# A hybrid mixer step on one core: the last RMSNorm of all rows moved into the last expert, into free weight slots

## The chip, the cores and the metric

One Trainium2 chip, one of its cores. The time is device microseconds of one launch of the whole program on that core; the median of the runs is what counts. A profile is one execution of the same program with the hardware profiler on.

## The reference, cut to what matters

One layer is computed for 1024 latent rows and 256 context rows of 1024 floats (all float32). After a mixer (Fourier and retention heads) comes an expert-choice MoE: each of 16 experts picks the 128 latent rows and 32 context rows with its highest gates, and its weighted output is added to these rows. A row can be picked by several experts or by none. Then every row is normalised once more.

```python
def rmsnorm(x, g):
    r = lax.rsqrt(jnp.mean(x * x, axis=-1, keepdims=True) + EPS)
    return (x * r) * g

gates, idx = lax.top_k(aff.T, cap)                 # per expert: cap rows
xs = ht[idx]
y = (silu(xs @ w_gate) * (xs @ w_up)) @ w_down * gates[..., None]
x = x + gate2 * zeros.at[idx].add(y)               # over 16 experts
y_prompt, y_sample = rmsnorm(xp, final_g), rmsnorm(xs, final_g)
```

## The kernel before, in words

The program is raw blocks, one after the other, each with a hand-written instruction list per engine and semaphores between them; every block ends with all engines meeting. Up to the router (the first 840 us) the rows are mixed, normalised and stored twice in device memory: `xn2` (input of the experts) and `acc` (the residual, to which expert outputs are added). The MoE block takes the rest but for the last 30 us.

In the MoE block an expert is 11 steps (`STEPS`) of 256 hidden columns. Per step SP loads three 1 MB weight tiles (gate, up, down) into one of four slots of `rawW` (`RING`, slot = step mod 4). ACT and DVE split the weights into a high and a low fp32r part (`gate_up_hi` L1205 and `gate_up_lo` L1210, `down_hi` L1527 and `down_lo` L1594), PE does gate and up (`gate_up`, L1420, and for context rows L1433), ACT applies SiLU (`sg` L1552, `sgc` L1558), DVE multiplies, PE transposes the hidden tile (`psT` L1463/1464), ACT and DVE split it (`hidden_hi` L1522, `hidden_lo` L1586), and PE does the down product one step late (`down`, L1446 and L1454), counted by the semaphore `f_d`. The down product of the last step of the last expert stands behind the loop, alone. Then ACT copies half of the context sums (`take_context_half` L1533), DVE applies the gates (`take_y`, L1607 to L1612), and POOL adds the 128 + 64 half rows into `acc` with two indirect DMAs that accumulate (`scatter`, L1662). POOL also gathers the input rows of the next expert into `xgS`/`xgP` (`gather`, L1655). The expert loop is `experts`: the first and the last expert are written out, the others are a hardware loop.

A last block then does the RMSNorm over ten tiles of 128 rows: SP loads each tile of `acc` (L1691) and `final_g` broadcast to all partitions (L1693); ACT squares and sums (L1708); POOL scales, adds EPS (L1714) and raises to -0.5 (L1716); DVE multiplies by that and by `final_g` (L1723); SP stores the tile (L1699).

Of the kernel before, what the change touches and what calls it, by code (L numbers as in the profile page):

```python
# [30 lines left out]
N = N_S + N_P  # L31
TS, TP = N_S // P, N_P // P
# [52 lines left out]
def build(nc, io):  # L85
    ctx = ExitStack()
    with ctx:
        sems = []

        def sem(name):  # L90
            sems.append(nc.alloc_semaphore(name=name))
            return sems[-1]

        def sb(name, shape, dt=F32, c=ctx):
            return c.enter_context(nc.sbuf_tensor(name, shape, dt))
# [836 lines left out]
        with ExitStack() as c:  # L932
# [26 lines left out]
            d_st = [sem("d_st0"), sem("d_st1")]  # L959
            d_tr, d_h2, d_lg, d_lc = sem("d_tr"), sem("d_h2"), sem("d_lg"), sem("d_lc")  # L960
            catv = catT.rearrange("(k p) n -> p k n", p=P)

            def schedule(eng, step):

# [247 lines left out]

        idxT = sb("idxT", [P, 48], I32)
        gT = sb("gT", [P, 48])
        with ExitStack() as c:
            mx = sb("mx", [P, T], F32, c)
            sm_ = sb("sm", [P, T], F32, c)
# [16 lines left out]
            with nc.Block() as block:  # L1234
# [39 lines left out]
                def _(dve):  # L1274
# [55 lines left out]
        with ExitStack() as c:  # L1330
# [17 lines left out]
            psS = ps("psS", [CS, 2, 512], c)  # L1348
            psP = ps("psP", [P, 512], c)
            X_AT, XS = 2, NK // 2  # L1350
            rows2 = [t.rearrange("n (a d) -> (n a) d", a=2) for t in (xn2, acc)]

            f_q, f_c = sem("f_q"), sem("f_c")
# [9 lines left out]

            f_si, f_yp, f_y, f_ys = sem("f_si"), sem("f_yp"), sem("f_y"), sem("f_ys")
            f_sc, f_free = sem("f_sc"), sem("f_free")

            def pair(t, e):

# [19 lines left out]
            with nc.Block() as block:  # L1388
                @block.sync
                def _(sp):  # L1390
                    sp.wait_ge(f_got, 32)

                    def load_down(e, i):
                        sp.wait_ge(f_d, STEPS * e + i - reuse(i) + 1)
                        load(sp, D_, e, i)

                    def body(e, first, last):
                        for i in range(STEPS):
                            s = STEPS * e + i
# [8 lines left out]
                    load_down(E - 1, STEPS - 1)  # L1408

                @block.tensor  # L1410
                def _(pe):
# [84 lines left out]
                def _(act):  # L1496
# [43 lines left out]
                    def body(e, first, last):  # L1540
                        for i in range(STEPS):
# [28 lines left out]
                    take_context_half(E)  # L1570

                @block.vector
                def _(dve):
# [29 lines left out]
                    def take_y(e):  # L1603
# [41 lines left out]
                    take_y(E)  # L1645

                @block.gpsimd
                def _(gp):
# [9 lines left out]
                    def scatter(e):  # L1658
# [4 lines left out]
                                                  compute_op=ALU.add).then_inc(f_sc, 16)  # L1663
                        gp.wait_ge(f_sc, 32 * e)

                    gather(0)

                    def body(e, first, last):
# [5 lines left out]
                            gp.sem_inc(f_free, 1)  # L1674

                    experts(gp, body)
                    scatter(E)

        with ExitStack() as c:  # L1680
            xf = sb("xf", [P, T, D], F32, c)
            gf = sb("gf", [P, D], F32, c)
            sq = sb("sqG", [P, 2, D], F32, c)
            ss, rs = sb("ssG", [P, T], F32, c), sb("rsG", [P, T], F32, c)
            g_g, g_x = sem("g_g"), a_x
            g_sq, g_ms, g_rs, g_y, g_out = sem("g_sq"), sem("g_ms"), sem("g_rs"), sem("g_y"), sem("g_out")
            with nc.Block() as block:  # L1687
                @block.sync
                def _(sp):
                    for t in range(T):  # L1690
                        sp.dma_start(xf[:, t, :], acc[t * P:(t + 1) * P, :]).then_inc(g_x[t], 16)  # L1691
                        if t == 0:
                            sp.dma_start(gf[:], io["final_g"].rearrange("(a d) -> a d", a=1).broadcast_to([P, D])  # L1693
                                         ).then_inc(g_g, 16)
                    for t in range(T):
                        sp.wait_ge(g_y, t + 1)
                        dst = (io["y_sample"][0, t * P:(t + 1) * P, :] if t < TS else
                               io["y_prompt"][0, (t - TS) * P:(t - TS + 1) * P, :])
                        sp.dma_start(dst, xf[:, t, :]).then_inc(g_out, 16)  # L1699
                    sp.wait_ge(g_out, 16 * T)  # L1700

                @block.scalar
                def _(act):
                    for t in range(T):
                        act.wait_ge(g_x[t], 32)
                        if t >= 2:
                            act.wait_ge(g_sq, t - 1)
                        act.activation(sq[:, t % 2, :], xf[:, t, :], ACT.Square, accum_out=ss[:, t:t + 1]).then_inc(g_sq, 1)  # L1708

                @block.gpsimd  # L1710
                def _(gp):
                    for t in range(T):
                        gp.wait_ge(g_sq, t + 1)
                        gp.tensor_scalar(ss[:, t:t + 1], ss[:, t:t + 1], 1.0 / D, EPS, ALU.mult, ALU.add).then_inc(g_ms, 1)  # L1714
                        gp.wait_ge(g_ms, t + 1)
                        gp.tensor_tensor(rs[:, t:t + 1], ss[:, t:t + 1], nhalf[:, 0:1], ALU.pow).then_inc(g_rs, 1)  # L1716

                @block.vector
                def _(dve):
                    dve.wait_ge(g_g, 16)  # L1720
                    for t in range(T):
                        dve.wait_ge(g_rs, t + 1)
# [24 lines left out]
```

## Time and profile before

| | us |
|---|---|
| median of 3 runs | 3174.97 (3174.19 to 3179.51) |
| the profiled execution, timed | 3178.7 |
| its span, first to last instruction | 3176.0 |
| PE busy of the span | 2915.9 (92%) |
| DVE busy | 1772.3 (56%) |
| ACT busy | 1574.4 (50%) |
| POOL busy | 435.5 (14%) |

The profile lists, per engine, what ran when, for how long, and what ended the idle time in front of it. Times in it are counted from the start of the span. A matmul's end is modelled; spans on POOL are rough. A register or semaphore instruction is not listed as busy.

### The profile page before, as it was taken

To read this page: it belongs to the slowest core of one execution; us is meant where nothing else is said; L and a number is where in the kernel's file an instruction comes from.
4 is the path that set the end of the run, shared out by engine and by line. 5 is a ranking of instruction groups with operands and counts; after the bars stand their busy time and mean duration, and the time that the engine had idled before them with its cause. 6 is when DMAs were issued, how large, how long until landed. Compare 5 with 4: busy or idle time off the path is not lost. (4 is left out here: it accounts for less than half of the span.)

```text
span 3176.0 us, 61303 instructions
## 1 busy us (share of the span) xinstructions
PE 2915.9 (92%) x23879; PEld 2200.5 (69%) x23879; DVE 1772.3 (56%) x2627; ACT 1574.4 (50%) x2473; POOL 435.5 (14%) x448
## 2 busy tenths in 40 slices
PE   5899998898399999999999999999999999999993
PEld 2799996587277767667676767667676767667772
DVE  2333331131667666666666666666666666666763
ACT  3322221133265656556565656556565656556652
POOL 3243331021201010101101010101101010101102
PEclk9999999898599999999999999999999999999996
DMA  9211102153577686868677686868678686868764
GB/s 385 76 41 35 34 17 78 50 175 119 196 238 253 232 293 218 295 228 270 229 262 261 229 290 210 295 232 272 230 256 266 229 291 205 295 234 274 249 237 147
DMA packets 483864, 668.99 MB, mean 211 GB/s; under 512 B 14689, under 2 KB 418993, under 8 KB 480562
## 3 DMA queue, kind: packets, MB, share of 16 engines
q1 hardware_dynamic: 476978, 644.45, 59.8%
q0 software_dynamic: 6656, 20.98, 2.6%
q8 instruction: 205, 3.36, 0.4%
q14 instruction: 25, 0.20, 0.0%
HBM read 633.39 MB, written 31.98 MB: 209 GB/s over the span
## 5 line engine op out<-in xcount | busy, mean ns | idle before, releaser
L1210 DVE TENSOR_TENSOR wGU_lo<-rawW,wGU_hi 128x1024 fp32r<-128x1024 f32 x700 | 824.9, 1218 | 74.3 <-ACT wGU_hi L1205 74.3
L1205 ACT ACTIVATE wGU_hi<-rawW 128x1024 fp32r<-128x1024 f32 x704 | 731.9, 1054 | 148.8 <-PE psGU L1420 139.7
L1420 PE MATMUL psGU<-wGU_hi,X_hi 128*128 128x512 f32 x1408 | 588.9, 418 | 54.4 <-issue 51.5
L1420 PE MATMUL psGU<-wGU_lo,X_hi 128*128 128x512 f32 x1408 | 568.4, 404 | 0.0
L1420 PE MATMUL psGU<-wGU_hi,X_lo 128*128 128x512 f32 x1408 | 567.7, 403 | 0.0
L1594 DVE TENSOR_TENSOR wD_lo<-rawW,wD_hi 128x1024 fp32r<-128x1024 f32 x352 | 415.2, 1220 | 63.1 <-ACT wD_hi L1527 63.1
L1586 DVE TENSOR_TENSOR hid_lo<-psT,hid_hi 128x256 fp32r<-128x256 f32 x176 | 74.5, 423 | 533.1 <-ACT hid_hi L1522 533.1
L1420 PEld LDWEIGHTS psGU<-wGU_hi,X_hi 128*128 128x128 f32 x1408 | 273.7, 194 | 124.5 <-issue 56.3
L1522 ACT ACTIVATE hid_hi<-psT 128x256 fp32r<-128x256 f32 x176 | 67.5, 384 | 576.6 <-PE psT L1464 576.2
L1527 ACT ACTIVATE wD_hi<-rawW 128x1024 fp32r<-128x1024 f32 x352 | 351.8, 1051 | 0.0
L1433 PE MATMUL psC<-rawW,Xc 128*32 128x128 f32 x11264 | 344.0, 274 | 0.0
L1433 PEld LDWEIGHTS psC<-rawW,Xc 128*32 128x32 f32 x11264 | 296.7, 110 | 64.4 <-issue 64.4
L1420 PEld LDWEIGHTS psGU<-wGU_hi,X_lo 128*128 128x128 f32 x1408 | 273.3, 194 | 65.1
L1420 PEld LDWEIGHTS psGU<-wGU_lo,X_hi 128*128 128x128 f32 x1408 | 274.2, 195 | 56.7
L1446 PE MATMUL psS<-wD_hi,hid_hi 128*128 128x512 f32 x704 | 238.4, 420 | 2.8 <-DVE wD_lo L1594 2.8
L1655 POOL DMA_INDIRECT xgS<-xn,gi x16 | 16.0, 1003 | 1610.4 <-DVE gi L1622 1583.2
L1446 PE MATMUL psS<-wD_lo,hid_hi 128*128 128x512 f32 x704 | 220.6, 395 | 0.0
L1446 PE MATMUL psS<-wD_hi,hid_lo 128*128 128x512 f32 x704 | 217.9, 391 | 0.0
L1662 POOL DMA_INDIRECT acc<-ysS,si x16 | 125.6, 7853 | 523.3 <-DVE ysP L1612 523.3
L1454 PE MATMUL psP<-rawW,hidc 128*32 128x512 f32 x1408 | 187.8, 605 | 0.0
L1446 PEld LDWEIGHTS psS<-wD_hi,hid_hi 128*128 128x128 f32 x704 | 118.9, 188 | 52.0 <-issue 37.6
L1446 PEld LDWEIGHTS psS<-wD_hi,hid_lo 128*128 128x128 f32 x704 | 132.7, 189 | 30.8
(235 smaller groups left out, 3673.2 us busy)
## 6 DMA issues: line engine op xcount, KB each, us to landing
rawW<-in_w_gate SPq DMA_DIRECT2D x176, 1024.0 KB, 5.5
rawW<-in_w_up SPq DMA_DIRECT2D x176, 1024.0 KB, 8.1
rawW<-in_w_down SPq DMA_DIRECT2D x176, 1024.0 KB, 8.4
wm<-in_w_mod SPq DMA_DIRECT2D x24, 1024.0 KB, 8.6
raw<-in_w_in SPq DMA_DIRECT2D x32, 192.0 KB, 2.5
rawc<-catT SPq DMA_DIRECT2D x10, 512.0 KB, 6.0
acc<-x SPq DMA_DIRECT2D x10, 512.0 KB, 2.7
xn<-xn SPq DMA_DIRECT2D x10, 512.0 KB, 4.1
```

What stands on the lines that cost most here:

```text
L1205: act.activation(hi, w, ACT.Copy).then_inc(f_whi, 1)
L1210: eng.tensor_tensor(lo, w, hi.bitcast(F32), ALU.subtract).then_inc(f_wlo, 1)
L1420: mm = pe.matmul(psGU[:].rearrange("p n f -> p (n f)"), X[a][:, k, :], wGU[b][:, k, :, :].rearrange("p n f -> p (n f)"), start=(k == 0 and ...
L1433: mm = pe.matmul(psC[at:at + CP, 0:P], Xc[:, k, :], w, start=(k == 0), stop=(k == NK - 1))
L1446: pe.matmul(psS[:, half, :], hid[a][:, f, :], wD[b][:, f, half * 512:(half + 1) * 512], start=(i == 0 and f == 0 and a == b), stop=(i == S ...
L1454: mm = pe.matmul(psP[at:at + CP, :], hidc[:, f, :], w, start=(i == 0), stop=(i == STEPS - 1), skip_group_check=True)
L1522: act.activation(hid[0][:].rearrange("p f c -> p (f c)"), psT[:, 0:2 * P], ACT.Copy).then_inc(f_hh, 1)
L1527: act.activation(wD[0][:, f, :], raw[:, i % RING, D_, f * D:(f + 1) * D], ACT.Copy).then_inc(f_dhi, 1)
L1586: dve.tensor_tensor(hid[1][:].rearrange("p f c -> p (f c)"), psT[:, 0:2 * P], hid[0][:].rearrange("p f c -> p (f c)").bitcast(F32), ALU.su ...
L1594: dve.tensor_tensor(wD[1][:, f, :], raw[:, i % RING, D_, f * D:(f + 1) * D], wD[0][:, f, :].bitcast(F32), ALU.subtract).then_inc(f_dlo, 1)
L1655: gp.indirect_dma_start(xg[r][:], None, table, bass.IndirectOffsetOnAxis(ap=gi[0:n, r:r + 1], axis=0)).then_inc(f_got, 16)
L1662: gp.indirect_dma_start(table, bass.IndirectOffsetOnAxis(ap=si[0:n, r:r + 1], axis=0), ys[r][:], None, compute_op=ALU.add).then_inc(f_sc, 16)
```

## The change

- The last block is gone. Its ten tiles are loaded by SP during the last expert, behind the last weight load, into slots of `rawW` that no later step uses: six into the slot of step 7 once its down product is done, four into that of step 8. They hold every row with the outputs of experts 0 to 14 added.
- ACT squares tiles 0 to 5 behind the SiLU of the last step, ahead of `hidden_hi` of that step, and tiles 6 to 9 behind `down_hi`; each square waits for the one ahead of it (one scratch tile, `xm`). POOL does the ten roots. DVE normalises the ten tiles in place behind `down_lo` and ahead of `take_y`; SP stores them.
- POOL gathers the last expert's 128 + 64 half rows from `acc` into `xgS`/`xgP` in that expert. After `take_y` DVE adds the expert's output to them, ACT squares them (the two halves of a context row meet by a swap of two columns, `fswap`), POOL makes the roots, DVE normalises, and two indirect DMAs that do not accumulate write these rows over those stored earlier; they wait until all ten stores have landed.
- `final_g` is loaded at the start of the MoE block (one full tile, two halves). One DVE instruction in the router block makes the row numbers of the context half rows in the output (`oT`). POOL clears the semaphores of the first stages at the start of the block that adds the mixer's output, so that their numbers can be used again.

```diff
+            nc.clear_and_free_semaphores([sm for sm in sems if sm.name.startswith(("b_", "c_"))])
...
+                    dve.tensor_scalar(oT[:], ti[0:2 * CP, 47:48], -2.0 * N_S, None, ALU.add)
...
+            SPARE = [LAST.index(STEPS - 4), LAST.index(STEPS - 3)]
+            SPARE_FROM = [STEPS * (E - 1) + STEPS - 3, STEPS * (E - 1) + STEPS - 2]
+            PER = 3 * NK * W_STEP // D
+            def row_buffer(t):
+                at = t % PER * D
+                return raw[:, SPARE[t // PER], :, :].rearrange("p n w -> p (n w)")[:, at:at + D]
...
                 def _(sp):
                     sp.wait_ge(f_got, 32)
+                    sp.dma_start(gf[:], io["final_g"].rearrange("(a d) -> a d", a=1).broadcast_to([P, D])).then_inc(g_g, 16)
+                    for a in range(2):
+                        half = io["final_g"][a * D // 2:(a + 1) * D // 2].rearrange("(a d) -> a d", a=1)
+                        sp.dma_start(gfP[a * CP:(a + 1) * CP, :], half.broadcast_to([CP, D // 2])).then_inc(g_g, 16)
...
                     load_down(E - 1, STEPS - 1)
+                    sp.wait_ge(f_sc, 32 * (E - 1))
+                    for t in range(T):
+                        if t % PER == 0:
+                            sp.wait_ge(f_d, SPARE_FROM[t // PER])
+                        sp.dma_start(row_buffer(t), acc[t * P:(t + 1) * P, :]).then_inc(g_x[t], 16)
+                    for t in range(T):
+                        sp.wait_ge(g_y, t + 1)
...
+                        sp.dma_start(dst, row_buffer(t)).then_inc(g_out, 16)
+                    sp.wait_ge(g_out, 16 * T)
...
+                    junk = xm[:, :, 0:CS]
+                    def square(t):
+                        act.wait_ge(g_x[t], 32)
+                        if t:
+                            act.wait_ge(g_sq, t)
+                        act.activation(junk, row_buffer(t).rearrange("p (k c) -> p k c", k=NK), ACT.Square,
+                                       accum_out=fs[:, t:t + 1]).then_inc(g_sq, 1)
...
+                            if last and i == STEPS - 1:
+                                for t in range(PER):
+                                    square(t)
                     experts(act, body)
                     hidden_hi(E - 1, STEPS - 1)
                     down_hi(E - 1, STEPS - 1)
+                    for t in range(PER, T):
+                        square(t)
                     take_context_half(E)
+                    act.wait_ge(g_sq, T)
+                    act.wait_ge(g_sum, 1)
+                    act.activation(junk, xg[0][:].rearrange("p (k c) -> p k c", k=NK), ACT.Square,
+                                   accum_out=fs[:, T:T + 1]).then_inc(h_sq, 1)
...
+                    def normalise(t):
+                        dve.wait_ge(g_rs, t + 1)
+                        row = row_buffer(t)
+                        dve.scalar_tensor_tensor(row, row, fr[:, t:t + 1], gf[:], ALU.mult, ALU.mult).then_inc(g_y, 1)
...
                     down_lo(E - 1, STEPS - 1)
+                    dve.wait_ge(g_g, 3 * 16)
+                    for t in range(T):
+                        normalise(t)
                     take_y(E)
+                    dve.wait_ge(f_got, 32 * (E + 1))
+                    dve.tensor_tensor(xg[0][:], xg[0][:], ys[0][:], ALU.add).then_inc(g_sum, 1)
...
                     experts(gp, body)
-                    scatter(E)
+                    gp.wait_ge(f_xt, XS * E)
+                    for r, n, table in ((0, CS, acc[:]), (1, 2 * CP, rows2[1])):
+                        gp.indirect_dma_start(xg[r][:], None, table, bass.IndirectOffsetOnAxis(ap=gi[0:n, r:r + 1], axis=0)
+                                              ).then_inc(f_got, 16)
+                    for t in range(T):
+                        gp.wait_ge(g_sq, t + 1)
+                        root(t, P, t + 1, g_ms, g_rs)
...
+                    gp.wait_ge(g_out, 16 * T)
+                    gp.wait_ge(h_y, 1)
+                    gp.indirect_dma_start(outS, bass.IndirectOffsetOnAxis(ap=gi[0:CS, 0:1], axis=0), xg[0][:], None
+                                          ).then_inc(h_out, 16)
+                    gp.wait_ge(h_y, 2)
+                    gp.indirect_dma_start(outP, bass.IndirectOffsetOnAxis(ap=oT[:], axis=0), xg[1][:], None
+                                          ).then_inc(h_out, 16)
+                    gp.wait_ge(h_out, 32)
-        with ExitStack() as c:
-            xf = sb("xf", [P, T, D], F32, c)
...
-                        dve.scalar_tensor_tensor(xf[:, t, :], xf[:, t, :], rs[:, t:t + 1], gf[:], ALU.mult,
-                                                 ALU.mult).then_inc(g_y, 1)
```

ACT, end of its list, before the change (the last step of the last expert and the last block; `sg`, `sgc` are the SiLUs, `hid_hi` and `wD_hi` the high parts for the last down product, `sqG` the squares of the last block):

```order
L1552 ACTIVATE sg<-psGU 128x256
L1558 ACTIVATE sgc<-psC 64x128
L1522 ACTIVATE hid_hi<-psT 128x256
L1527 ACTIVATE wD_hi<-rawW 128x1024 x2
L1533 ACTIVATE yp<-psP 64x512
L1388 UNCONDITIONAL_BRANCH
L1702 UNCONDITIONAL_BRANCH
L1708 ACTIVATE sqG,ssG<-xf 128x1024 x10
```

and of the change (rows of `acc` in the free slots are `rawW`, the sums `fs`):

```order
L1602 ACTIVATE sgc<-psC 64x128
L1576 ACTIVATE xm,fs<-rawW 128x8x128 x6
L1557 ACTIVATE hid_hi<-psT 128x256
L1562 ACTIVATE wD_hi<-rawW 128x1024 x2
L1576 ACTIVATE xm,fs<-rawW 128x8x128 x4
L1568 ACTIVATE yp<-psP 64x512
L1622 ACTIVATE xm,fs<-xgS 128x8x128
L1626 ACTIVATE xm,fs<-xgP 64x4x128
L1630 ACTIVATE fswap<-fs 32x1 x2
```

Six squares now stand between the last SiLU and `hid_hi`, four behind `wD_hi`, and four small instructions for the last expert's rows at the end.

DVE, end of its list, of the change (`wD_lo` is the low part for the last down product, `ysS` and `ysP` the last expert's output, `xgS` and `xgP` its rows of `acc`; before, the ten instructions on row tiles stood behind `ysP`, in the last block, and those on `xgS` and `xgP` were not there):

```order
L1655 TENSOR_TENSOR wD_lo<-rawW,wD_hi 128x1024 x2
L1679 SCALAR_TENSOR_TENSOR rawW<-rawW,fr,gf 128x1024 x10
L1668 SCALAR_TENSOR_TENSOR ysS<-psS,gc,gate2S 128x1024
L1671 TENSOR_TENSOR ysP<-psP,yp 64x512
L1673 SCALAR_TENSOR_TENSOR ysP<-ysP,gc,gate2P 64x512
L1716 TENSOR_TENSOR xgS<-xgS,ysS 128x1024
L1718 TENSOR_TENSOR xgP<-xgP,ysP 64x512
L1720 SCALAR_TENSOR_TENSOR xgS<-xgS,fr,gf 128x1024
L1722 SCALAR_TENSOR_TENSOR xgP<-xgP,fr,gfP 64x512
```

The ten tiles stand ahead of `ysS`, and four instructions have come behind `ysP`.

## Rows read from the trace of the kernel before

**Rows 1.** The page: its first line.

```profile
span 3176.0 us, 61303 instructions
```

**Rows 2.** Timeline, last down product to `take_y`: start, us, engine, line, operation [idle before].

```profile
3120.10 0.38 ACT L1522 ACTIVATE hid_hi<-psT 128x256 fp32r<-128x256 f32 x1 [4.21 <-PE psT L1464]
...
3121.46 2.36 DVE L1594 TENSOR_TENSOR wD_lo<-rawW,wD_hi 128x1024 fp32r<-128x1024 f32 x2 [0.39 <-ACT wD_hi L1527]
...
3129.67 1.28 DVE L1607 SCALAR_TENSOR_TENSOR ysS<-psS,gc,gate2S 128x1024 f32<-128x1024 f32 x1 [5.85 <-PE psP L1454]
3131.58 0.74 DVE L1612 SCALAR_TENSOR_TENSOR ysP<-ysP,gc,gate2P 64x512 f32<-64x512 f32 x1
```

**Rows 3.** Timeline: last scatter, first load of the last block.

```profile
3133.09 1.56 POOL L1662 DMA_INDIRECT acc<-ysS,si  x1 [121.88 <-DVE ysP L1612]
3134.96 1.43 POOL L1662 DMA_INDIRECT acc<-ysP,si  x1 [0.30 <-issue]
3145.95 0.34 SPq L1691 DMA_DIRECT2D xf<-acc  x1
```

**Rows 4.** DMA issues, 3133 to 3137 us: KB each, us from issue to landing.

```profile
acc<-ysP,si POOLq DMA_INDIRECT x1, 5.3
```

**Rows 5.** Stretches: us, busy PE, PEld, DVE, ACT, POOL, PEclk, DMA share, GB/s.

```profile
3140.00:3146.00 6.00, 0.00 (x0) 0.00 (x0) 0.00 (x0) 0.00 (x0) 0.00 (x0) 0.50 0.00 0
```

**Rows 6.** Timeline of the last block: its first root, one tile's pace, the last tile.

```profile
3150.66 0.19 POOL L1714 TENSOR_SCALAR ssG<-ssG 128x1 f32<-128x1 f32 x1 [14.27 <-ACT sqG L1708]
...
3157.04 1.06 ACT L1708 ACTIVATE sqG<-xf 128x1024 f32<-128x1024 f32 x1 [0.37 <-DMA xf<-acc]
3157.16 1.28 DVE L1723 SCALAR_TENSOR_TENSOR xf<-xf,rsG,gf 128x1024 f32<-128x1024 f32 x1 [0.71 <-POOL rsG L1716]
3157.21 1.28 POOL L1714 TENSOR_SCALAR ssG<-ssG 128x1 f32<-128x1 f32 x1
3158.27 1.06 ACT L1708 ACTIVATE sqG<-xf 128x1024 f32<-128x1024 f32 x1
3158.57 0.55 POOL L1716 TENSOR_TENSOR rsG<-ssG,nhalf 128x1 f32<-128x1 f32 x1
3159.16 1.28 DVE L1723 SCALAR_TENSOR_TENSOR xf<-xf,rsG,gf 128x1024 f32<-128x1024 f32 x1 [0.72 <-POOL rsG L1716]
...
3171.16 1.28 DVE L1723 SCALAR_TENSOR_TENSOR xf<-xf,rsG,gf 128x1024 f32<-128x1024 f32 x1 [0.72 <-POOL rsG L1716]
```

**Rows 7.** DMA issues: the last store (3172 to 3176 us); loads of row tiles.

```profile
y_prompt<-xf SPq DMA_DIRECT2D x1, 512.0 KB, 3.1
...
xf<-acc SPq DMA_DIRECT2D x10, 512.0 KB, 8.9
```

**Rows 8.** Timeline: down products of steps 7 and 8 of the last expert end.

```profile
3094.07 1.07 PE L1454 MATMUL psP<-rawW,hidc 128*32 128x512 f32 x8
...
3106.25 1.06 PE L1454 MATMUL psP<-rawW,hidc 128*32 128x512 f32 x8
```

**Rows 9.** Timeline at the first gather.

```profile
839.37 0.17 DVE L1574 COPY gi<-idxT 128x2 int32<-128x2 int32 x1 [0.32 <-PEq L1234]
840.49 1.22 POOL L1655 DMA_INDIRECT xgS<-xn,gi  x1 [27.14 <-DVE gi L1574]
845.71 0.69 PE L1472 MATMUL psX<-ident,xgS 128*128 128x128 f32 x2 [7.02 <-DMA xgP<-xn,gi]
```

**Rows 10.** Timeline: the scatter in the last expert's first step, POOL and DVE.

```profile
3001.18 8.29 POOL L1662 DMA_INDIRECT acc<-ysS,si  x1 [126.22 <-DVE ysP L1612]
...
3007.94 0.27 DVE L1635 TENSOR_TENSOR hfc<-sgc,psC 64x128 f32<-64x128 f32 x1
```

**Rows 11.** Timeline: POOL and PE in the mixer-output block; SP's next weight load.

```profile
627.73 11.59 POOL L1149 TENSOR_SCALAR diag<-ident,modT 128x128 f32<-128x128 f32 x16 [137.76 <-POOLq L734]
646.60 0.60 PE L1026 MATMUL opsD<-diag,ones 128*128 128x128 f32 x4
...
867.24 0.37 SPq L1190 DMA_DIRECT2D rawW<-in_w_gate  x1
```

More of the change, by code:

```diff
@@ L1214, in build @@
         gT = sb("gT", [P, 48])
+        oT = sb("oT", [2 * CP, 1], I32)
         with ExitStack() as c:
@@ L1350, in build @@
             X_AT, XS = 2, NK // 2
+            gf, gfP = sb("gf", [P, D], F32, c), sb("gfP", [2 * CP, D // 2], F32, c)
+            fs, fr = sb("fs", [P, T + 2], F32, c), sb("fr", [P, T + 2], F32, c)
+            fswap = sb("fswap", [2 * CP, 1], F32, c)
+            SPARE = [LAST.index(STEPS - 4), LAST.index(STEPS - 3)]
[4 more added lines that the diff above has]
+                return raw[:, SPARE[t // PER], :, :].rearrange("p n w -> p (n w)")[:, at:at + D]
             rows2 = [t.rearrange("n (a d) -> (n a) d", a=2) for t in (xn2, acc)]
@@ L1365, in build @@
             f_sc, f_free = sem("f_sc"), sem("f_free")
+            g_g, g_x = sem("g_g"), a_x
+            g_sq, g_ms, g_rs, g_y, g_out = sem("g_sq"), sem("g_ms"), sem("g_rs"), sem("g_y"), sem("g_out")
+            g_sum, g_swap, g_two, g_add = sem("g_sum"), sem("g_swap"), sem("g_two"), sem("g_add")
+            h_sq, h_ms, h_rs, h_y, h_out = sem("h_sq"), sem("h_ms"), sem("h_rs"), sem("h_y"), sem("h_out")
+            outS = io["y_sample"][0]
+            outP = io["y_prompt"][0].rearrange("n (a d) -> (n a) d", a=2)
             def pair(t, e):
@@ L1408, in _ @@
                     load_down(E - 1, STEPS - 1)
+                    sp.wait_ge(f_sc, 32 * (E - 1))
[5 more added lines that the diff above has]
+                        sp.wait_ge(g_y, t + 1)
+                        dst = (io["y_sample"][0, t * P:(t + 1) * P, :] if t < TS else
+                               io["y_prompt"][0, (t - TS) * P:(t - TS + 1) * P, :])
+                        sp.dma_start(dst, row_buffer(t)).then_inc(g_out, 16)
+                    sp.wait_ge(g_out, 16 * T)
                 @block.tensor
@@ L1569, in _ @@
                     down_hi(E - 1, STEPS - 1)
+                    for t in range(PER, T):
+                        square(t)
                     take_context_half(E)
+                    act.wait_ge(g_sq, T)
+                    act.wait_ge(g_sum, 1)
+                    act.activation(junk, xg[0][:].rearrange("p (k c) -> p k c", k=NK), ACT.Square,
+                                   accum_out=fs[:, T:T + 1]).then_inc(h_sq, 1)
+                    act.wait_ge(g_sum, 2)
+                    act.wait_ge(h_sq, 1)
+                    act.activation(junk[0:2 * CP, 0:NK // 2, :], xg[1][:].rearrange("p (k c) -> p k c", k=NK // 2), ACT.Square,
+                                   accum_out=fs[0:2 * CP, T + 1:T + 2]).then_inc(g_swap, 1)
+                    act.wait_ge(g_swap, 1)
+                    for a in range(2):
+                        op = act.activation(fswap[a * CP:(a + 1) * CP, :], fs[(1 - a) * CP:(2 - a) * CP, T + 1:T + 2], ACT.Copy)
+                    op.then_inc(g_two, 1)
                 @block.vector
@@ L1644, in _ @@
                     down_lo(E - 1, STEPS - 1)
+                    dve.wait_ge(g_g, 3 * 16)
+                    for t in range(T):
+                        normalise(t)
                     take_y(E)
+                    dve.wait_ge(f_got, 32 * (E + 1))
+                    dve.tensor_tensor(xg[0][:], xg[0][:], ys[0][:], ALU.add).then_inc(g_sum, 1)
+                    dve.wait_ge(f_ys, E)
+                    dve.tensor_tensor(xg[1][:], xg[1][:], ys[1][:], ALU.add).then_inc(g_sum, 1)
+                    dve.wait_ge(h_rs, 1)
+                    dve.scalar_tensor_tensor(xg[0][:], xg[0][:], fr[:, T:T + 1], gf[:], ALU.mult, ALU.mult).then_inc(h_y, 1)
+                    dve.wait_ge(h_rs, 2)
+                    dve.scalar_tensor_tensor(xg[1][:], xg[1][:], fr[0:2 * CP, T + 1:T + 2], gfP[:],
+                                             ALU.mult, ALU.mult).then_inc(h_y, 1)
                 @block.gpsimd
@@ L1664, in scatter, with root @@
                         gp.wait_ge(f_sc, 32 * e)
+                    def root(at, n, count, ms, rs):
+                        gp.tensor_scalar(fs[0:n, at:at + 1], fs[0:n, at:at + 1], 1.0 / D, EPS, ALU.mult, ALU.add).then_inc(ms, 1)
+                        gp.wait_ge(ms, count)
+                        gp.tensor_tensor(fr[0:n, at:at + 1], fs[0:n, at:at + 1], nhalf[0:n, 0:1], ALU.pow).then_inc(rs, 1)
                     gather(0)
@@ L1676, in _ @@
                     experts(gp, body)
-                    scatter(E)
-        with ExitStack() as c:
-            xf = sb("xf", [P, T, D], F32, c)
[L1682 to L1711, printed above, removed]
@@ L1715, in _ @@
[L1715 to L1722, printed above, removed]
-                        dve.scalar_tensor_tensor(xf[:, t, :], xf[:, t, :], rs[:, t:t + 1], gf[:], ALU.mult,
-                                                 ALU.mult).then_inc(g_y, 1)
+                        root(t, P, t + 1, g_ms, g_rs)
@@ new lines, in _ @@
+                    gp.wait_ge(h_sq, 1)
+                    root(T, P, 1, h_ms, h_rs)
+                    gp.wait_ge(g_two, 1)
+                    gp.tensor_tensor(fs[0:2 * CP, T + 1:T + 2], fs[0:2 * CP, T + 1:T + 2], fswap[:], ALU.add).then_inc(g_add, 1)
+                    gp.wait_ge(g_add, 1)
+                    root(T + 1, 2 * CP, 2, h_ms, h_rs)
+                    gp.wait_ge(g_out, 16 * T)
+                    gp.wait_ge(h_y, 1)
+                    gp.indirect_dma_start(outS, bass.IndirectOffsetOnAxis(ap=gi[0:CS, 0:1], axis=0), xg[0][:], None
+                                          ).then_inc(h_out, 16)
```

1 line of the change is left out of this document (removed).

## The prediction

> **What bounds it now.** I read the page first. The span is 3176.0 us [rows 1], and PE is busy for 92% of it; the expert steps, where PE works, are not touched by the change, so whatever it gains or loses lies in the stretch where PE has run dry. The second view is the timeline from the last SiLU on. There one engine after the other works while the rest wait: the last down product, `take_y` until 3132.3 [rows 2], the scatter, whose second DMA starts at 3135.0 [rows 3] and lands 5.3 us later [rows 4], at 3140.3. Then nothing: the view by stretches shows no engine busy and no DMA traffic from 3140 to 3146 [rows 5], and the first load of the last block stands at 3145.95 [rows 3]. These 5.65 us belong to the closing of a block on whose POOL queue DMAs had just landed; no row names the instruction. Where POOL issues none just ahead of the end, closing is short: the last tile is ready at 3172.44 [rows 6], its store lands 3.1 us behind its issue [rows 7], at about 3175.6, and the span ends at 3176.0.
>
> The last block takes 30 us for 10 tiles. Its pace is not that of the loads but of two engines that exclude each other: DVE starts a tile at 3157.16 and the next at 3159.16, 2.00 us apart, though it is busy 1.28 of them [rows 6]. In between POOL's scaling of one column, 0.19 us when DVE is idle, starts with DVE's instruction and takes the same 1.28; then its power takes 0.55 with DVE waiting [rows 6]. So a root costs DVE 0.72 us a tile.
>
> **The change, part by part.** All times are in the profiled execution (span 3176.0 us); at the end the difference goes to the median of 3174.97.
>
> *Ahead of the last expert.* POOL's clearing of semaphores stands ahead of 16 instructions that end at 639.3, while PE asks for them at 646.6 [rows 11]: 7 us of cover for three small instructions, so 0. The row-number instruction in the router lies on the path; the nearest small DVE row is 0.17 us [rows 9]: +0.2. SP's three new loads of 640 KB stand at the block's start, where SP's next weight load is due only at 867.2 [rows 11], 22 us after the first gather is there [rows 9]: 0. If that cover were gone, they would cost some 1.5 us. POOL's gather from `acc` has over 100 us of the last expert for itself: 0.
>
> *Loads of the ten tiles.* The down products of steps 7 and 8 end at 3095.1 and 3107.3 [rows 8]. A tile landed 8.9 us after its issue in the median, with ten in flight [rows 7]. So tiles 0 to 5 are there by about 3105 and tiles 6 to 9 by about 3115, and no weight load is queued behind them on SP. ACT wants the first at 3115.9: 0, with 10 us in hand.
>
> *Six squares ahead of `hid_hi`.* ACT ends its last SiLU at 3115.9 and is idle for 4.21 us until the transposes are done, at 3120.1 [rows 2]. Squares followed each other at 1.23 us [rows 6]; here each also waits for the one before, for which I add 0.05 (bounds 0 and 0.15, the gap between POOL's two dependent instructions being 0.08 [rows 6]). Six take 7.7, so `hid_hi` starts at 3123.6, not 3120.1: 3.5 us late, and with it `wD_lo`, which ended at 3123.8 [rows 2] and now ends at 3127.3, and the last down product, done at 3133.1, not 3129.6. POOL's first six roots run beside this, with DVE mostly idle.
>
> *Ten normalisations ahead of `take_y`.* Tiles 0 to 5 have their roots: 6 by 1.23 us, from 3127.3 to 3134.7. Squares 6 to 9 follow `wD_hi` and end by 3131. Their roots are asked of POOL while DVE runs without a pause. Either POOL gets in only when DVE stops, and then four tiles go at 2.00, or it gets in between and DVE waits 0.72 four times; both give `take_y` a start at 3142.9. Without any exclusion it would be 3127.3 + 10 x 1.23 = 3139.6; I take 3142.9, since rows 6 show the exclusion on the same pair of operations. The down product was done at 3133.1, so this order holds the last expert's own rows back for 9.8 us.
>
> *The last expert's rows.* From 3142.9: `take_y` 2.65 [rows 2], to 3145.55; the addition of 128x1024 at 1.2, half of the pair of `wD_lo` [rows 2], to 3146.75; its square 1.23, to 3148.0; POOL's root 0.19 + 0.55 and three hand-overs of 0.1, to 3149.05; DVE 1.28 for it, to 3150.35. The context half runs beside that up to POOL, which is shut out until DVE is through; then it adds the two half sums (0.19 to 0.55, the two one-column rows; I take 0.35) and makes the root, with hand-overs 1.4, to 3151.75. DVE's last 0.74 lies beside the start-up of the first DMA.
>
> *Two plain scatters.* The trace has none. The gather, as long in bytes and as many rows, took from DVE's index at 839.54 to PE's start at 845.71, 6.2 us [rows 9]; the accumulating scatter took from 3132.32 to 3140.3, 8.0 us [rows 2 to 4]. A plain write neither reads nor adds at its target, so I take 6.2 and keep 8.0 for the range. From the first issue at 840.49 to PE's start it is 5.2 us [rows 9]. The Trainium skill (DMA: Bandwidth & Descriptors, "Anatomy of one DMA — SWDGE (gpsimd) path") gives about 2.0 us plus the bytes at 436 GB/s for a DMA issued from POOL, which as an estimate is 3.5 us for the 640 KB of both; the sum would be 1.7 us shorter by it. The gather's row is the longer one and is measured here, so it goes into the sum. Landing is at 3157.95. The ten stores in front of it, which must have landed, end 3.1 us behind the last normalised tile [rows 7], at 3146, and hide.
>
> *Closing.* The block again ends right behind landed DMAs of POOL, so I set 5.65 us [rows 3 to 5]: the span ends at 3163.6. Lower bound: the 0.4 us behind the last store of the kernel before [rows 1, 6, 7].
>
> **Sum.** 3163.6 - 3176.0 + 0.2 = -12.2 us; from the median of 3174.97 that is **3162.8 us**, 0.4% faster. A change below 0.2%, 6.3 us, can hardly be told from none in this kernel. Put as a gain: 30 us of last block, the old scatter and its closing go; 3.5 us of late `hid_hi`, 9.8 us of `take_y` held back, 8.9 us for the rows' own norm, 6.2 us of scatter and 5.65 us of closing stand at the end in their place.
>
> **Rivals.**
> 1. *No second closing gap.* The gap could belong to the accumulating DMAs or to the start of the next block, which no longer exists. For it: it is seen once. Against it: the two block ends without fresh POOL DMAs show none, whether a block follows or not (at the router's end DVE's next instruction waited 0.32 us [rows 9], at the program's end it is 0.4). Then 5.25 less: 3157.5.
> 2. *No exclusion for the four late roots.* DVE never waits: 3.3 less, 3159.5. Against it stand rows 6.
> 3. *No change: the write is starved.* The first DMA of a scatter took 8.29 us, not 1.56, where DVE ran without a pause, and ended 1.3 us after DVE paused at 3008.2 [rows 3, 10]. If DVE's last instructions did this to the new scatter, 6.7 us come on top: 3169.5, within 0.2% of before. Against it: DVE has one instruction of 0.74 us left then. The Trainium skill (SBUF — State Buffer, "Who interferes with whom") infers that a `tensor_tensor` with both inputs in SBUF does not stall the descriptors that GpSimd makes for its own DMAs; by that the rival would have no chance at all, but rows 10 speak against it, so it keeps one.
> 4. *Slower: ACT blocked by a late tile.* The six squares stand ahead of `hid_hi` on ACT. If tile 5 lands after 3122.3, when ACT reaches it, every microsecond delays the whole end one for one. Slower than before by 0.2% needs 18.5 us more, a landing after 3141. That takes the scatter of expert 14, which SP waits for, to land after 3130. Its first DMA ended at 3009.5 [rows 10], the second starts 0.3 later and lands within 5.3 or so [rows 3, 4]: 3015. So the margin is over 100 us, and only a slow read could do it: 3182 and above.
>
> **How the numbers follow.** Forecast 0.70, rival 1 0.12, rival 2 0.06, rival 3 0.08, rival 4 0.04. Faster by over 0.2% takes the first three, 0.88; same 0.08; slower 0.04. The range runs from rival 1 with 1 us for the spread of runs, 3156.5, to the forecast with the upper bounds of scatter (+1.8), squares (+0.6) and half sums (+0.2) and 1.6 us of spread, 3167. It leaves out rivals 3 and 4 and the case that 1 and 2 both hold, 0.15 together.
>
> **What would show it.** In the new timeline: `hid_hi` of the last step at 3123 to 3124 (same origin); DVE's tiles at 1.2 us first and 2.0 at the end; `ysS` near 3143; the two output DMAs near 3152 to 3154, landing by 3158; then a quiet stretch of over 5 us up to the end. Wrong would be: `ysS` before 3140, no quiet stretch, a first output DMA of 3 us or more, or expert steps that are longer than before, for which I see no cause.

## The result, and the profile after

| | before | after |
|---|---|---|
| median, us | 3175.28 (3174.19 to 3179.51) | **3148.2** (3147.9 to 3151.44) |
| ratio | | 0.9917, 95% interval 0.9902 to 0.9932 |
| the profiled execution, timed | 3178.7 | 3151.44 |

The change makes the kernel 27 us faster, 0.8%. The forecast was 3162.8, and its range ended at 3156.5: right in its sign, too small by more than half. The page of the kernel after begins:

```profile
span 3149.0 us, 61321 instructions
```

The timeline of its tail (start, us, engine, line, operation [idle before]), from `hid_hi` of the last step on. It answers to [rows 2, 3, 6]:

```profile
3114.45 0.38 ACT L1557 ACTIVATE hid_hi<-psT 128x256 fp32r<-128x256 f32 x1
...
3115.80 2.36 DVE L1655 TENSOR_TENSOR wD_lo<-rawW,wD_hi 128x1024 fp32r<-128x1024 f32 x2 [0.39 <-ACT wD_hi L1562]
...
3118.08 12.04 DVE L1679 SCALAR_TENSOR_TENSOR rawW<-rawW,fr,gf 128x1024 f32<-128x1024 f32 x10
3118.30 1.47 POOL L1748 TENSOR_TENSOR fr<-fs,nhalf 128x1 f32<-128x1 f32 x1
...
3119.85 0.76 POOL L1746 TENSOR_SCALAR fs<-fs 128x1 f32<-128x1 f32 x1
...
3123.70 0.59 ACT L1568 ACTIVATE yp<-psP 64x512 f32<-64x512 f32 x1 [2.22 <-PE psP L1489]
...
3130.04 1.28 DVE L1668 SCALAR_TENSOR_TENSOR ysS<-psS,gc,gate2S 128x1024 f32<-128x1024 f32 x1
...
3135.42 0.55 POOL L1748 TENSOR_TENSOR fr<-fs,nhalf 128x1 f32<-128x1 f32 x1
...
3136.01 1.28 DVE L1720 SCALAR_TENSOR_TENSOR xgS<-xgS,fr,gf 128x1024 f32<-128x1024 f32 x1 [1.58 <-POOL fr L1748]
3136.40 0.93 POOL L1771 TENSOR_TENSOR fs<-fs,fswap 64x1 f32<-64x1 f32 x1 [0.43 <-ACT fswap L1630]
...
3137.69 0.54 POOL L1748 TENSOR_TENSOR fr<-fs,nhalf 64x1 f32<-64x1 f32 x1
...
3138.44 1.54 POOL L1776 DMA_INDIRECT y_sample<-xgS,gi  x1 [0.21 <-issue]
3140.29 0.91 POOL L1779 DMA_INDIRECT y_prompt<-xgP,oT  x1 [0.30 <-issue]
```

The shape is the one foretold: ten tiles ahead of `ysS`, which is held back (the down product was done by 3123.7, when `yp` starts), then the last expert's rows, two DMAs and a quiet end. The second DMA lands 2.9 us behind its issue, at 3143.2 (DMA issues):

```profile
y_prompt<-xgP,oT POOLq DMA_INDIRECT x1, 2.9
```

From there to the end nothing runs (stretches; us, busy PE, PEld, DVE, ACT, POOL, PEclk, DMA share, GB/s), as in [rows 5]:

```profile
3143.00:3149.00 6.00, 0.00 (x0) 0.00 (x0) 0.00 (x0) 0.00 (x0) 0.00 (x0) 0.50 0.00 0
```

But the tail has not all of the gain. The `hidden_lo` of the first step in expert 1 and in expert 15 cuts a run into front, 14 middle experts and tail. Before:

```profile
1011.47 0.41 DVE L1586 TENSOR_TENSOR hid_lo<-psT,hid_hi 128x256 fp32r<-128x256 f32 x1
...
3000.34 0.41 DVE L1586 TENSOR_TENSOR hid_lo<-psT,hid_hi 128x256 fp32r<-128x256 f32 x1
```

After:

```profile
1011.98 0.41 DVE L1647 TENSOR_TENSOR hid_lo<-psT,hid_hi 128x256 fp32r<-128x256 f32 x1
...
2991.60 0.41 DVE L1647 TENSOR_TENSOR hid_lo<-psT,hid_hi 128x256 fp32r<-128x256 f32 x1
```

| us, profiled pair | before | after | difference | foretold |
|---|---|---|---|---|
| front, to expert 1 | 1011.5 | 1012.0 | +0.5 | +0.2 |
| experts 1 to 14 | 1988.9 | 1979.6 | **-9.2** | 0 |
| tail, from expert 15 | 175.7 | 157.4 | **-18.3** | -12.4 |

Some 1.2 us of the tail's 18.3 belong to this one profiled execution of the kernel before: by the clock records the end of its last expert had 6.8 us at half the granted clock. Nine of ten other profiles with the old tail had 3.4 there and a tail of 174.2 to 174.8 us; the tenth, b_pad, had 6.8 and 175.7.

So two questions: why 9 us in a loop whose instructions are the same, and why 6 us more in the tail.

In the loop the view of waits (window 990 to 2990: engine, line, what for; us in total, times, longest) has one large PE entry, the first product of an expert, waiting for "issue", that is, for nothing that the profile shows. Before:

```profile
PE psGU L1420 <- issue: 51.5, 13, 4.9
```

After:

```profile
PE psGU L1455 <- issue: 45.0, 13, 4.8
```

Thirteen times is once for each return of the hardware loop. One of them in the timeline of the kernel before, PE:

```profile
1558.88 0.27 PE L1464 MATMUL psT<-ident,hfc 64*128 64x64 f32 x1
1564.08 0.79 PE L1420 MATMUL psGU<-wGU_hi,X_hi 128*128 128x512 f32 x1 [4.93 <-issue]
```

and the stretches behind it:

```profile
1564.10:1567.50 3.40, 3.40 (x8) 2.72 (x9) 0.00 (x0) 0.32 (x1) 0.00 (x0) 0.50 1.03 352
...
1570.90:1574.30 3.40, 3.40 (x71) 2.67 (x70) 2.51 (x4) 2.48 (x4) 0.00 (x0) 1.00 0.68 216
```

### The profile page after: what moved, and what is told of

Same layout as the page of the kernel before. It is cut to its first block, busy times and chain, and to the rows that moved or that the text cites. A ratio compares the mean times of both kernels' runs of the same rounds, so it can differ in the third digit from the quotient of the medians.

```text
span 3149.0 us, 61321 instructions
## 1 busy us (share of the span) xinstructions
PE 2912.1 (92%) x23879; PEld 2195.9 (70%) x23879; DVE 1775.9 (56%) x2632; ACT 1576.7 (50%) x2479; POOL 438.3 (14%) x455
## 4 chain that ended last, share of the span: by engine, by line
PE 70%; issue 2%; DVE 1%; ACT 1%; POOL 0%; DMA 0%; ACTq 0%; POOLq 0%
PE psGU L1455 33%; PE psS L1481 16%; PE psC L1468 10%; PE psP L1489 6%; PE psT L1498 2%; PE psT L1499 1%; PE psX L1507 1%; PE psX L1508 0%; DVE rawW L1679 0%; ACT xm L1576 0%; ACT xm L1538 0%; DMA xgP<-xn,gi 0%; DVE wGU_lo L1211 0%; DVE wD_lo L1655 0%; POOL y_sample L1776 0%
## 5 line engine op out<-in xcount | busy, mean ns | idle before, releaser
L1481 PEld LDWEIGHTS psS<-wD_lo,hid_hi 128*128 128x128 f32 x704 | 132.8, 189 | 29.1
```

The source lines that it names most:

```text
L1481: pe.matmul(psS[:, half, :], hid[a][:, f, :], wD[b][:, f, half * 512:(half + 1) * 512], start=(i == 0 and f == 0 and a == b), stop=(i == S ...
```

## The experiments

### Is the loop's gain the loop's returns?

b_unroll and a_unroll write the 14 middle experts out, in the kernel before and in the changed one:

```diff
-                with eng.Fori(1, E - 1) as e:
-                    body(e, False, False)
+                for e in range(1, E - 1):
+                    body(e, False, False)
```

> The kernel before with the 14 middle experts written out instead of a hardware loop; nothing else. Theory R (return): in the trace before, the step that ends an iteration takes 18.4 us on the mean against 12.2 for the same step where nothing returns, because PE has to wait 2.9 to 4.9 us for its first instruction after the jump and then runs for 3.4 or 6.8 us at the lower clock; written out, 13 x 6.2 = 81 us go: about 3094 us. Rival S (steps): if that time is not the jump's but the step's (last step of an expert), written out it stays, and the time is 3175.

> The changed kernel with the 14 middle experts written out; nothing else. Theory R: of the 27 us that the change brought, about 18 are the tail's and about 9 come from shorter waits at the 13 jumps. Without jumps, this kernel is 18 us faster than the kernel before with its experts written out, about 3076 us. Rival T: all 27 us belong to the tail or to the steps; then the difference between the two written-out kernels is 27 us, 3067.

Measured: 3091.75 (3090.96 to 3093.08) and 3074.09 (3071.88 to 3074.87). Without the returns the kernel before is 81 us faster, the changed one 74; the view of waits has no such entry left. The two differ by 17.7 us, most of it the tail's share (174.2 against 157.4 us in the profiles). The first line of the page and two `hidden_lo` rows of the timeline, of b_unroll:

```profile
span 3089.9 us, 57210 instructions
...
1008.04 0.41 DVE L1586 TENSOR_TENSOR hid_lo<-psT,hid_hi 128x256 fp32r<-128x256 f32 x1
...
2915.68 0.41 DVE L1586 TENSOR_TENSOR hid_lo<-psT,hid_hi 128x256 fp32r<-128x256 f32 x1
```

and of a_unroll:

```profile
span 3070.1 us, 57228 instructions
...
1005.22 0.41 DVE L1647 TENSOR_TENSOR hid_lo<-psT,hid_hi 128x256 fp32r<-128x256 f32 x1
...
2912.67 0.41 DVE L1647 TENSOR_TENSOR hid_lo<-psT,hid_hi 128x256 fp32r<-128x256 f32 x1
```

1907.64 and 1907.45: without returns the middle experts are alike. All of the loop's gain was at the returns. Waits and half of the half-clock time, 51.5 and 31.6 us, make 83 us, beside the 81.2 that writing out took from these experts.

### Chance?

a_again is the changed kernel unaltered.

> The changed kernel itself once more, for more executions. Written out, the two kernels differ by 17.7 us; before scatters by 13 us from run to run (3165.5 to 3178.9) through the waits at the jumps. Theory C (chance): the 9 us beyond the tail came from the few executions taken: mean of before less 17.7, about 3156. Theory P (part of the change): the change shortens the waits at the jumps for good: 3148 again, within 2.

3151.25 (3144.78 to 3154.16), ratio 0.9929 (0.9916 to 0.9943), PE's waits again 45.0 us. Single runs spread over 9 us, and the median lies between the two figures, nearer to P's; with the same 45.0 us in a second profile I took the shorter returns for systematic and looked for their cause.

### Which part of the change shortens the returns?

Each kernel here is the kernel before with one edit. First the clearing of semaphores alone (b_clear), and PE's code moved by waits on a semaphore long there (b_pad):

```diff
+            nc.clear_and_free_semaphores([sm for sm in sems if sm.name.startswith(("b_", "c_"))])
```

```diff
+                    for _ in range(64):
+                        pe.wait_ge(a_const, 16)
```

> The kernel before with the clearing of the first stages' semaphores alone, nothing else of the change: the later stages' semaphores get other numbers, POOL's code is six instructions longer, SP's, PE's, ACT's and DVE's code is the same. If the loop's 9 us come with that: 3166. If not: 3175 within 2.

> The kernel before with 32 more instructions on PE ahead of the expert loop (waits that are long met, where PE waits anyway for the first gather): they move the loop's code on PE by 32 places and cost nothing themselves. Theory L (layout): how long PE waits at a jump depends on where the loop's first instruction lies in the pieces in which code is loaded; then the time moves by several us, either way. Rival: the waits depend on what else is in the DMA queues; then 3175 within 2.

Then all that the change adds ahead of the loop (b_front), and its parts: the three loads of `final_g` (b_loads), SP waits in their place (b_spwait), the row-number instruction (b_row).

> The kernel before with all that the change adds ahead of the expert loop (semaphore clearing, row numbers, three loads of final_g), and its old tail. PE's waits at the 13 loop returns add up to 51 us in the kernel before and 45 in the changed one. Theory F (a part ahead of the loop makes the returns shorter): the sum falls to about 45 us and the time to 3168 +-2. Theory G (it is the new tail, or chance): 51 to 52 us and 3173 +-2, as the kernel before beside it.

> The kernel before with the three loads of final_g ahead of the loop, and their tiles, alone. Theory H (the loads, their tiles or SP's code that moves with them make the returns shorter): PE's waits at the 13 returns near 45 us, time 3166 +-2, as in b_front. Theory I (the row-number instruction, which moves DVE's code, does it): 51 to 52 us and 3173 +-2.

> The kernel before with three waits of SP on a semaphore that is already there, in the place of the three loads: SP's code behind them moves, nothing else does. Theory K (it is the place of SP's code): waits near 45 us, 3166 +-2. If b_loads is shorter and this is not: the loads or the tiles do it, 51 to 52 us and 3173 +-2 here.

> The kernel before with the row-number instruction of DVE alone. Theory I: waits near 45 us, 3166 +-2. Theory H: 51 to 52 us, 3173 +-2.

And that last one in halves: DVE waits in its place (b_dvewait), its tile without the instruction (b_tile), and a larger tile (b_tile16).

```diff
         gT = sb("gT", [P, 48])
+        oT = sb("oT", [2 * CP, 1], I32)
```

> The kernel before with two waits of DVE on a semaphore that is already there, in the place of the row-number instruction; no tile. Theory M (DVE's code behind it moves): PE's waits at the 13 returns near 45 us, 3165 +-2. Theory N (the later tiles move in on-chip memory): 50 to 52 us, 3173 +-2.

> The kernel before with the tile of the row numbers, never written. Theory M: PE's waits 50 to 52 us, 3173 +-2. Theory N: near 45 us, 3165 +-2.

> The kernel before with an unused tile of 64 bytes in each partition in the place of 4. Theory Q (the shift of the later tiles by a few bytes does it, a 64-byte step keeps their place against each other): PE's waits at the 13 returns 50 to 52 us, 3173 +-2. Theory R2 (any tile there does it): near 45 us, 3167 +-2.

| | median, us | ratio to the kernel before run beside it, 95% | PE's waits at the 13 returns, us |
|---|---|---|---|
| b_clear | 3175.36 | 0.9991 to 1.0017 | 51.1 |
| b_pad | 3178.73 | 1.0005 to 1.0032 | 52.2 |
| b_loads | 3172.51 | 0.9997 to 1.0018 | 50.3 |
| b_spwait | 3174.09 | 0.9999 to 1.0017 | 50.8 |
| b_dvewait | 3174.13 | 0.9987 to 1.0004 | 50.5 |
| **b_front** | 3165.80 | 0.9963 to 0.9981 | 45.2 |
| **b_row** | 3165.03 | 0.9966 to 0.9986 | 45.2 |
| **b_tile** | 3167.72 | 0.9967 to 0.9987 | 44.8 |
| **b_tile16** | 3151.22 | 0.9915 to 0.9942 | 44.4 |

The waits fall into two groups without overlap: 50.3 to 52.2 us in the kernels without the row numbers' tile, 44.4 to 46.0 in those with it (45.0 in both profiles of the changed kernel, 46.0 in a_early below). The time at half clock does not split so: 56 to 63 us in the first group, 58 to 62 in the second, b_tile16 apart. So of the 9.2 us the 6.5 are the change's, and the 2.8 can be chance. The rows of b_dvewait and b_tile, view of waits:

```profile
PE psGU L1422 <- issue: 50.5, 13, 5.0
```

```profile
PE psGU L1421 <- issue: 44.8, 13, 4.0
```

So neither the instruction nor code that moves is needed: **four bytes per partition**, never written, declared behind the weight slots and ahead of the other tiles of the experts, take 7.8 us off (3175.47 to 3167.72). The tiles of b_loads, 4 and 2 KB a partition, do nothing, but they are declared behind all others. Theories G, H, K and M fall; F and N hold, I as to the edit but not in its reason. Theory L's waits didn't change (52.2 us), though b_pad is 0.2% slower: in its profile the front is 3.2 us longer than in that of before, and the middle experts are 1.1 us shorter. b_tile16 went further than either theory: the unused tile of 64 bytes alone gains 23 us, nearly as much as the whole change. Its waits are those of b_tile; what is new is the step. Steps 1 and 10 of its last expert:

```profile
2985.17 0.43 DVE L1587 TENSOR_TENSOR hid_lo<-psT,hid_hi 128x256 fp32r<-128x256 f32 x1 [2.64 <-ACT hid_hi L1523]
...
3094.37 0.42 DVE L1587 TENSOR_TENSOR hid_lo<-psT,hid_hi 128x256 fp32r<-128x256 f32 x1 [4.18 <-ACT hid_hi L1523]
```

109.20 us for nine steps; before it is 109.61:

```profile
3010.91 0.43 DVE L1586 TENSOR_TENSOR hid_lo<-psT,hid_hi 128x256 fp32r<-128x256 f32 x1 [2.69 <-ACT hid_hi L1522]
...
3120.52 0.42 DVE L1586 TENSOR_TENSOR hid_lo<-psT,hid_hi 128x256 fp32r<-128x256 f32 x1 [4.16 <-ACT hid_hi L1522]
```

That is 0.05 us a step, some 8 us over 16 experts. The granted clock gives some 7 us more: in the 10 us behind each of the 13 returns, the time at half clock adds up to 49.9 us in b_tile16 and 63.2 before, and I again count half of the difference as lost work, an estimate. With the 7.1 us of shorter waits these make some 22 of the 23. That the place of the later tiles does all this is inferred from the order of the declarations; the trace has no addresses. Why the packet starts earlier and the steps are shorter stays open.

### The tail: where do 6 us come from?

From here the written-out kernels serve, in which nothing moves at the returns. Their medians still differ by a few us for what happens ahead of the experts (the first `hidden_lo` stood at 867.3 to 873.8 in these profiles), so the tail is read from the profile, from the last expert's first `hidden_lo` to the end: 157.4 us in a_unroll, 174.2 in b_unroll.

au_sq_late moves squares 0 to 5 behind `down_hi`, so that DVE meets every root while it is being made:

```diff
-                            if last and i == STEPS - 1:
-                                for t in range(PER):
-                                    square(t)
...
-                    for t in range(PER, T):
+                    for t in range(T):
                         square(t)
```

> On the changed kernel written out (3074.1): tiles 0 to 5 are squared behind the high parts of the last down product, as 6 to 9 are, so that hid_hi is on time. Theory E: roots that come late cost DVE 2.00 us a tile as in the last block of before, because DVE waits for the root and POOL for DVE's instruction: hid_hi 3.4 us earlier, ysS 5.5 us later, 3079.6. Rival F: POOL's roots cost DVE nothing, the pace is ACT's 1.24: ysS 2 us earlier, 3072.

3081.81 (3078.76 to 3082.5), tail 162.5: 7.7 us slower by the medians, 5.1 by the tail; theory E, which foretold 5.5. Its DVE timeline:

```profile
3040.75 1.29 DVE L1676 SCALAR_TENSOR_TENSOR rawW<-rawW,fr,gf 128x1024 f32<-128x1024 f32 x1 [0.72 <-POOL fr L1745]
3042.76 1.29 DVE L1676 SCALAR_TENSOR_TENSOR rawW<-rawW,fr,gf 128x1024 f32<-128x1024 f32 x1 [0.72 <-POOL fr L1745]
```

and POOL's:

```profile
3040.80 1.29 POOL L1743 TENSOR_SCALAR fs<-fs 128x1 f32<-128x1 f32 x1
3042.17 0.55 POOL L1745 TENSOR_TENSOR fr<-fs,nhalf 128x1 f32<-128x1 f32 x1
```

Here all ten tiles go at 2.00, as in [rows 6]; in the changed kernel all ten go at 1.20. The idle 0.72 of DVE is a wait for the root's semaphore; DVE's own instruction grows no longer. What grows beside it is POOL's scaling, from 0.19 to 1.29 us, and this makes the root late.

au_early moves work into the idle time: squares 0 to 2 ahead of the last SiLU, tiles 0 to 2 ahead of `hidden_lo`, 3 to 7 ahead of `take_y`, 8 and 9 behind the additions. a_early is the same edit with the hardware loop.

```diff
+                            if end:
+                                for t in range(3):
+                                    square(t)
...
-                                for t in range(PER):
+                                for t in range(3, PER):
                                     square(t)
...
+                    dve.wait_ge(g_g, 3 * 16)
+                    for t in range(3):
+                        normalise(t)
...
-                    for t in range(T):
+                    for t in range(3, 8):
                         normalise(t)
...
+                    for t in range(8, T):
+                        normalise(t)
```

> On the changed kernel written out (3074.1): squares 0 to 2 move to ACT's idle time ahead of the last SiLU, 3 to 5 stay behind it, DVE normalises tiles 0 to 2 ahead of hid_lo, 3 to 7 ahead of take_y, 8 and 9 behind the additions. If hid_hi's delay (3.4 us) and take_y's being held back (6.3 us) are on the path, both go: about 3065. If only hid_hi's delay counts: 3070.7. If neither: 3074.

> The changed kernel, loop not written out, with squares 0 to 2 ahead of the last SiLU, DVE's tiles 0 to 2 ahead of hidden_lo and tiles 8 and 9 behind the additions. Theory P (the returns are shorter in every kernel with the new tail): the changed kernel's 3150 less the 6.3 us that the same edit gave in the written-out version, 3143.5 +-2, PE's waits at the returns again near 45 us. Theory C (they shift with anything in the program): the waits leave 44 to 46 us in either direction and the time leaves 3141 to 3146.

au_early: 3067.77 (3065.28 to 3070.08), tail 149.9, 7.5 us less than a_unroll; most, not all, of both gains. a_early: **3140.9** (3139.93 to 3145.24), ratio 0.9889 (0.9872 to 0.9905), faster than every other kernel with the loop kept. It is 2.6 below theory P's figure and 0.1 below theory C's span, and its waits of 46.0 stand at the edge of that span, so it does not settle between the two.

Two kernels ask for the closing. au_sp_end lets SP, not POOL, wait for the last two DMAs; au_noscatter has no such DMAs.

```diff
+                    sp.wait_ge(h_out, 32)
...
-                    gp.wait_ge(h_out, 32)
```

> On the changed kernel written out (3074.1): SP, not POOL, waits for the last two DMAs to land; POOL goes to the end of the block as soon as it has issued them. If the 5.5 us of closing are POOL's own work and take as long whether its DMAs have landed or not, they now start 2 us earlier: 3072.2. If closing starts from the landing of POOL's DMAs: 3074 within 0.7.

> The written-out changed kernel without its last two output DMAs: the rows of the last expert keep the outputs of experts 0 to 14 alone. Beside 3074.1 us with them. Theory N (closing is long because DMAs of POOL have just landed): the DMAs' 4.2 us beyond the last instruction of DVE and the 5.4 us of closing go, 3064.5. Theory O (closing is long wherever POOL has issued DMAs in the block, however long ago): only the DMAs go, 3069.9.

au_noscatter: 3073.22 (3069.82 to 3075.77). The median lies outside both theories, 0.9 below a_unroll's; the tail, free of what happens ahead of it, is 153.1, 4.3 us less than a_unroll's, which is theory O. Its last instruction, and the stretch behind it, in which no DMA of POOL can have just landed:

```profile
3064.80 0.74 DVE L1722 SCALAR_TENSOR_TENSOR xgP<-xgP,fr,gfP 64x512 f32<-64x512 f32 x1 [0.98 <-POOL fr L1748]
```

```profile
3065.80:3071.00 5.20, 0.00 (x0) 0.00 (x0) 0.00 (x0) 0.00 (x0) 0.00 (x0) 0.50 0.00 0
```

au_sp_end: 3075.37 (3073.68 to 3077.13), which read by the medians is no gain; but its tail is 155.3, 2.1 us less, and its front was longer in the profiled run. In the trace's records, behind the views, these stretches are a drain of POOL: 5.30 us before, 5.46 after, 5.29 in au_noscatter. In au_sp_end it begins ahead of POOL's second DMA and ends 5.5 us behind the end of POOL's last issue. So the closing runs from POOL's own last work, beside the landing if POOL doesn't wait for it. Theory N of au_noscatter, which is the prediction's own reason, falls. That the drain is long because POOL has issued DMAs in the block, as theory O has it, is not shown: no run has this block without them.

au_both has both edits.

> The written-out changed kernel with both edits of the tail: squares and normalisations moved forward (149.9 us from the last expert's first hidden_lo to the end, beside 157.4), and SP in POOL's place waiting for the last two output DMAs (155.3). If they add up: 147.8 us in that stretch, and some 3065.7 as the time. If the second is swallowed: 149.9 and 3067.8.

3066.85 (3065.24 to 3068.51), tail 147.7: they add up. Ratio 0.9662 (0.9649 to 0.9675), the fastest of all, though no surer than au_early by its runs. A changed kernel with the 64-byte tile was not tried.

## Why the prediction was wrong in size

- **"The expert steps, where PE works, are not touched by the change, so whatever it gains or loses lies in the stretch where PE has run dry."** This step failed, and by 9.2 of 14.8 us. The steps are indeed the same, but 13 loop returns lay between them, with 51.5 us of PE waiting that the view of waits shows in one row and that I had not read. The waits fell to 45.0 us, and b_tile shows that the row numbers' unused tile is enough for this; the prediction priced that instruction by its 0.17 us and left its tile at nothing.
- **Ten normalisations, "both give `take_y` a start at 3142.9".** Failed: from the first tile to `ysS` it took 11.96 us, not 15.6. Rows 6 show DVE idle for 0.72 beside POOL's work, and I read it as a mutual exclusion. Rival 2 was the true case, and the rows had the evidence: POOL's scaling stretched to the length of DVE's instruction, while DVE's own 1.28 never grew. Here POOL pays, its two operations going from 0.19 and 0.55 to 0.76 and 1.47, and DVE pays nothing so long as its roots are ready. The sign of being wrong that the prediction gave came: `ysS` stands at 3130.04, and at 3138.8 even with the 8.7 us that the last expert began earlier. The term's own sum is also not quite right: four tiles at 2.00 give 3142.7 and four waits of 0.72 give 3142.5, so 0.2 to 0.4 us of it has no row.
- **Six squares ahead of `hid_hi`.** Right: 3.1 us late (counted from the expert's first `hidden_lo`), foretold 3.5.
- **The last expert's rows.** Right in mechanism, 8.2 us from `ysS` to the last root, foretold 8.85.
- **Two plain scatters.** Mis-sized: 4.95 us from there to the landing, foretold 6.2 by the gather's row. The prediction's other estimate, 3.5 us by the Trainium skill (DMA: Bandwidth & Descriptors, "Anatomy of one DMA — SWDGE (gpsimd) path"), was 1.45 us too short.
- **Closing.** The term was right (5.8 us, foretold 5.65), its reason failed: not fresh landings but POOL's drain, 5.29 us in au_noscatter with no DMA of POOL for 126 us. Rival 1 is out.
- **Rivals 3 and 4.** The first output DMA took 1.54 us, so DVE's end starved nothing; ACT ran through the six squares without waiting for a load.
- Together: the tail's terms come to -5.9 us against the forecast (-0.4 and -0.1 around `hid_hi`, -3.6, -0.7, -1.25, +0.15) and the loop's to -9.2; the front gives 0.3 back, and -14.8 is left. With the tail alone mis-sized the time would have stood near 3157, at the lower end of the range.

## What to carry to other kernels

Read the view of waits for loop returns before calling a loop untouched: 13 of them cost 74 to 81 us here, and writing the loop out gave more than the change did. A tile that nothing uses changed the time here, so before a gain below 1% is put down to an edit, give the old kernel the same tile, unused, and time it. When two engines go at one pace, look whose instruction grew longer before charging both. And let GpSimd finish its work in the last block early: here its drain, run beside the landing, gave 2.1 us.

## What was not expected of the hardware

- A return of the hardware loop cost PE 2.6 to 5.1 us of waiting. Behind it the granted clock was half the full one for 2.8 to 6.2 us, in all but one of the 169 returns in 13 profiles. Written out, an expert took 136.25 us, in the loop 139 to 144.
- An unused tile of 4 bytes a partition shortened the returns (51 to 45 us in total), one of 64 bytes also the steps (12.18 to 12.13 us): 0.2% and 0.7% of the kernel.
- POOL's drain at the end of the MoE block, the only one in which it issues DMAs, took 5.3 to 5.5 us behind its last work, even with 126 us since POOL's last DMA; it was 0.66 in the last block before.
